# Dividing the neighbourhood attention's weights by their row sums: on GpSimd before the transposes, in place of diagonal matrices and ones products

## The chip, the cores and the metric

The kernel runs on one NeuronCore of a Trainium2 chip, as one launch. The metric is the time of one execution on the device, in microseconds (us). The five engines of a core run their own instruction queues in program order and wait for each other by semaphores: PE (TensorE, matmuls into PSUM), DVE (VectorE), ACT (ScalarE), POOL (GpSimd) and SP (which here issues most DMAs). GpSimd works only on SBUF in this kernel; PSUM is read by DVE and ACT.

## The reference, cut to what matters

The whole program is a small network: two layers that mix neighbourhood attention, differential attention and a convolution, and then feed-forward blocks with two other mixers. The change touches only the neighbourhood attention of the two layers, and there only the softmax's division:

```python
T, CTX, GRID_W, heads, dh = 512, 256, 64, 6, 64      # window of 8 rows x 16 columns
s_loc = einsum('bnqhd,bnkhd->bhnqk', q, k_window) + bias      # masked outside the window
s_ctx = einsum('bnqhd,bkhd->bhnqk', q, k_context)
p = softmax(concatenate([s_loc, s_ctx], axis=-1), axis=-1)
o = einsum('bhnqk,bnkhd->bnqhd', p[..., :nk], v_window) + einsum('bhnqk,bkhd->bnqhd', p[..., nk:], v_context)
y = concatenate([o * silu(gate), ...]) @ w_out
```

Layer 0 also computes a dense attention of the 256 context tokens over themselves in the same way; layer 1 does not. All of it is in float32.

## The kernel before, in words

`NaStage` does this attention, once in each of the two layers (`na0`, `na1`). Its work is cut into steps k = (p, b): p is one of three pairs of heads, and b is a block of 128 queries. Blocks b = 0 to 3 are latent queries against 256 keys of their window and the 256 context keys; b = 4 (layer 0 only) is the context, 256 queries against 256 keys, which has the same size of 128 partitions x 512 for each of the pair's two heads (i = 0, 1). Layer 0 has 15 steps, layer 1 has 12.

One step goes round all engines:

- **scores** (`scores_pe`, PE): queries times keys into two PSUM banks, 4 matmuls in the program.
- **max** (`max_dve`, DVE): adds the bias to the window's half and writes it to SBUF (`self.s[k % 3]`), and takes the row maxima. Its first instruction on the two heads is L1337 for b < 4, L1345 for b = 4.
- **exp** (`exp_act`, ACT, L1301): exponentials into `self.s[k % 3]`, with row sums in the small array `st`.
- **sums** (`sums_dve`, DVE, L1358 and L1360, or L1362 for b = 4): one over the row sums.
- **diag** (`diag_pool`, POOL, L1373): the identity matrix times one over the row sums, a diagonal matrix for each head (four 128x128 instructions for b = 4, else two).
- **turn** (`turn_pe`, PE, through the helper at L354): 8 transposes of the undivided weights, keys onto partitions, into banks 4 and 5.
- **copy** (`copy`, ACT L1285 for head 0, DVE L1287 for head 1): to SBUF, `self.pt[k % 2]`.
- **values** (`values_pe`, PE, through the helper at L345): first the ones products (a matrix of ones times the diagonal, which spreads one over the row sum of each query over 64 partitions in bank 7), then values times weights into bank 6.
- **out** (`out_dve`, DVE, L1387 and L1389): at the end of the latent blocks (b = 3) and for the context (b = 4), gate times bank 7, then times bank 6.

The order on each engine is written out by hand. PE's round k is values(k - 3), turn(k - 2), scores(k + 1). DVE's round k is max(k), sums(k - 1), out(k - 3), copy(k - 2). ACT's is copy(k - 2), exp(k). POOL does diag(k) for one k after another, and after k = 3 issues the DMA of the third pair's bias table. `self.s` has three buffers, `self.pt` has two, the score banks are two pairs. After the last step a fence has ACT, DVE and POOL wait for all others; PE goes on with the projections of the next stage, `LateStage`.

In the program a float32 product is one instruction; the trace shows two records for each.

Of the kernel before, what the change touches and what calls it, by code (L numbers as in the profile page):

```python
# [18 lines left out]
P = 128  # L19
# [171 lines left out]
def build(nc, ins, out_dram):  # L191
# [6 lines left out]
    with ctx:  # L198
# [946 lines left out]
        class NaStage:  # L1145
# [5 lines left out]
            def __init__(self, l, total, place, mix, norm, mod):  # L1151
                self.l, self.total, self.mix, self.tag, self.mod = l, total, mix, f"na{l}", mod
                self.norm = norm
                self.kT, self.qT, self.v = place.take(3, TA), place.take(3, TA), place.take(9, NA_W)
                self.s = [place.take(2, T) for _ in range(3)]
                self.pt = [place.take(2, T) for _ in range(2)]
                side = mix[:, 3:9, :].rearrange("p a b -> p (a b)")
                self.bias = [side[:, i * 1536:(i + 1) * 1536].rearrange("p (i b n) -> p i b n", i=2, b=3)
                             for i in range(2)]
                self.diag = [side[:, 3072 + i * T:3072 + (i + 1) * T].rearrange("p (a b) -> p a b", a=4) for i in range(3)]  # L1160
                names = lambda g: [(f"w_in{l}", i) for i in IN_PIECE[g]]
                self.k_of = Project(names(0), P, norm, TA)
                self.v_of = ByColumns(Project(names(1), P, norm, TA), self.v, [self.s[n][:, 0, :] for n in range(2)])
                self.g_of = Project(names(5), P, norm, total)
                self.q_of = Project(names(4), P, norm, total)
                self.steps = [(p, b) for p in range(3) for b in range(5 if total == TA else 4)]
                self.n = len(self.steps)
# [55 lines left out]
            def turn_pe(self, q, e, k):  # L1223

                for i in range(2):
                    q.wait_ge(*at(self.tag, "exp", k, i))
                    if k:
                        q.wait_ge(*at(self.tag, "copied", k - 1, i))
                    for j in range(4):
                        t = turned(e, banks[4 + i][:, j * P:(j + 1) * P], self.s[k % 3][:, i, j * P:(j + 1) * P])  # L1230
                    t.then_inc(*sig("na_turned", self.tag, "turned", k, i))

            def values_pe(self, q, e, k):
# [4 lines left out]
                    q.wait_ge(*at(self.tag, "out", k - 1))  # L1238
                if b == 4:
                    q.wait_ge(*at(self.tag, "out", k - 1))  # L1240
                q.wait_ge(*at(self.tag, "diag", k))
                for u in range(2 if b == 4 else 1):
                    c = (u if b == 4 else b) * P
                    for i in range(2):
                        mm(e, banks[7][64 * i:64 * i + 64, c:c + P], ones[:, 0:64],
                           self.diag[k % 3][:, 2 * i + u, :], True, True)
                tiles = self.TILES[b] + (7, 8) if b < 4 else (7, 8, 7, 8)
                for j, n in enumerate(tiles):
                    for i in range(2):
# [112 lines left out]
                    e.reciprocal(st[:, 12:16], st[:, 8:12]).then_inc(*sig("softmax"))  # L1362
                also(self.tag, "one over", k)

            def diag_pool(self, q, e, k):
                p, b = self.steps[k]
                st = self.st(k)
                q.wait_ge(*at(self.tag, "one over", k))
                if k >= 3:
                    q.wait_ge(*at(self.tag, "o", k - 3))  # L1370
                for n in range(2 if b < 4 else 4):
                    at4 = 2 * n if b < 4 else n
                    e.tensor_scalar(self.diag[k % 3][:, at4, :], ident, st[:, 12 + n:13 + n], None, MUL).then_inc(  # L1373
                        *sig("na_diag", self.tag, "diag", k))

            def out_dve(self, q, e, k):
                p, b = self.steps[k]
                if b < 3:
                    return
                q.wait_ge(*at(self.tag, "o", k))  # L1380
                if b == 3:
                    m = self.by_rows(self.mix[:, p, 0:T])
                    over, o = self.by_columns(banks[7]), self.by_columns(banks[6])
                else:
                    m = self.mix[:, p, T:TA]
                    over, o = banks[7][:, 0:TC], banks[6][:, 0:TC]
                e.tensor_tensor(m, over, m, MUL).then_inc(*sig("na_scaled"))  # L1387
                q.wait_ge(*last())
                e.tensor_tensor(m, o, m, MUL).then_inc(*sig("na_out", self.tag, "out", k))  # L1389


# [7 lines left out]
            def pool(self, q, e):  # L1399
                for p in range(2):  # L1400
                    q.wait_ge(*at(self.norm.tag, "lo", (len(spans(TA))) * DT - 1))
                    self.fetch_bias(q, e, p)
                for project in (self.k_of, self.v_of.p, self.g_of, self.q_of):
                    for n in project.pieces:
                        rest_of_weights(q, e, n)
                for k in range(self.n):
                    self.diag_pool(q, e, k)
                    if k == self.steps.index((0, 3)):
                        self.fetch_bias(q, e, 2)

# [2085 lines left out]
```

## Time and profile before

| | |
|---|---|
| median of 3 runs | 3389.8 us (3381.35 to 3390.28) |
| the profiled execution | 3391.12 us, of which its span of instructions 3389.3 us |
| PE busy, of the span | 3190.4 us, 94% |
| DVE busy | 1669.4 us, 49% |
| ACT busy | 1212.3 us, 36% |
| POOL busy | 748.7 us, 22% |
| the chain that ended last | PE 86%, DVE 7%, ACT 4%, POOL 1% |
| steps of `na0` | from 161.5 to 221.1 us of the span |
| steps of `na1` | from 743.3 to 792.3 us of the span |

The span is the stretch from the first to the last instruction of one profiled execution; the times in the rows below count from its start. The chain that ended last is followed back from the last instruction, at each step to what released it. The two stages of the change are 109 us of the 3389.3 us. Busy shares over the whole span say little on them: what counts is who waits for whom between 161.5 and 221.1 us and between 743.3 and 792.3 us.

### The profile page before, as it was taken

How to read it: one execution, taken by the hardware profiler on the slowest of the kernel's cores; microseconds unless marked ns; L12 is line 12 of the kernel's file. 1: busy time of each engine (PE TensorE's matmuls, PEld its weight loads, DVE VectorE, ACT ScalarE, POOL GpSimd, SP SyncE). 2: the span in 40 equal slices, each digit the busy share in tenths (PEclk: the TensorE clock that was granted, in tenths of full speed). 3: DMA queues.
4: the chain of work that ended last, by engine and by line, in shares of the span. 5: the costliest groups of instructions: out<-in, count | busy, mean ns of one | idle time of the engine just before them, and what ended most of it. 6: DMA issues, size and time to landing. Idle time of an engine off the chain costs nothing.

```text
span 3389.3 us, 39869 instructions
## 1 busy us (share of the span) xinstructions
PE 3190.4 (94%) x16156; PEld 2509.4 (74%) x16156; DVE 1669.4 (49%) x2507; ACT 1212.3 (36%) x2068; POOL 748.7 (22%) x578
## 2 busy tenths in 40 slices
PE   6999988899989999989899999999999999999998
PEld 4877667677767788867788778887888775578886
DVE  2256564426674534456665553446444425564344
ACT  3242265433273322232443332233222325542222
POOL 3234302334504000056332300001000343220000
PEclk8999999999999999999899999999999999999999
DMA  5213201221102232222000133232232231022322
GB/s 227 94 53 113 100 24 31 78 68 54 59 13 79 96 97 99 87 96 81 14 7 1 62 100 106 92 98 84 87 107 87 81 106 38 1 93 88 111 84 79
DMA packets 77575, 260.55 MB, mean 77 GB/s; under 512 B 8400, under 2 KB 9552, under 8 KB 76240
## 3 DMA queue, kind: packets, MB, share of 16 engines
q1 hardware_dynamic: 76528, 253.28, 22.8%
q0 software_dynamic: 864, 4.72, 0.4%
q8 instruction: 129, 2.11, 0.3%
q14 instruction: 54, 0.44, 0.0%
HBM read 255.87 MB, written 2.10 MB: 76 GB/s over the span
## 4 chain that ended last, share of the span: by engine, by line
PE 86%; DVE 7%; ACT 4%; POOL 1%; issue 1%; DMA 1%; SPq 0%; ACTq 0%; DVEq 0%; POOLq 0%
PE banks L345 84%; PE banks L354 2%; DVE area L576 1%; POOL w_lo L336 1%; DMA area<-in_w_mod 1%; DVE x_lat L579 1%; DVE small L1797 0%; DVE area L1741 0%; DVE area L1779 0%; ACT area L434 0%; POOL w_late L336 0%; ACT area L437 0%; ACT w_hi L326 0%; POOL area L410 0%; DVE area L494 0%
## 5 line engine op out<-in xcount | busy, mean ns | idle before, releaser
L345 PE MATMUL banks<-area,w_hi 128*128 128x512 f32 (+4 forms) x5896 | 1770.8, 383 | 22.7 <-ACT area L532 7.4
L345 PEld LDWEIGHTS banks<-area,w_hi 128*128 128x128 f32 (+2 forms) x5896 | 1078.5, 188 | 287.9 <-issue 22.6
L345 PE MATMUL banks<-area,w_lo 128*128 128x512 f32 (+4 forms) x2948 | 1120.2, 381 | 0.0
L345 PEld LDWEIGHTS banks<-area,w_lo 128*128 128x128 f32 (+2 forms) x2948 | 554.8, 188 | 118.8
L345 PE MATMUL banks<-area,w_late 128*128 128x512 f32 (+2 forms) x2316 | 580.8, 399 | 28.9 <-ACT area L532 14.8
L345 PEld LDWEIGHTS banks<-area,w_late 128*128 128x128 f32 (+1 forms) x2316 | 436.1, 191 | 146.9 <-ACT area L532 18.1
L326 ACT ACTIVATE w_hi<-w_raw 128x1024 fp32r<-128x1024 f32 (+2 forms) x361 | 349.7, 972 | 544.9 <-PE banks L345 416.3
L345 PE MATMUL banks<-area,area 64*128 64x256 f32 (+11 forms) x3464 | 419.0, 334 | 59.7 <-DMA area<-in_w_mod 15.9
L410 POOL TENSOR_TENSOR area<-area,area 128x512 f32<-128x512 f32 (+1 forms) x102 | 140.4, 1379 | 1475.2 <-ACT area L395 1473.5
L345 PEld LDWEIGHTS banks<-area,area 128*128 128x128 f32 (+4 forms) x3464 | 335.1, 183 | 134.1 <-issue 54.8
L336 POOL TENSOR_TENSOR w_lo<-w_raw,w_hi 128x1024 fp32r<-128x1024 f32 (+1 forms) x133 | 305.0, 2295 | 401.4 <-ACT w_hi L326 401.4
L336 DVE TENSOR_TENSOR w_lo<-w_raw,w_hi 128x1024 fp32r<-128x1024 f32 (+1 forms) x228 | 263.4, 1156 | 158.6 <-ACT w_hi L326 158.6
L969 ACT ACTIVATE area<-area 128x512 fp32r<-128x512 f32 x88 | 55.7, 632 | 419.1 <-DVE area L1000 419.1
L345 PE MATMUL banks<-area,const 128*128 128x512 f32 (+7 forms) x542 | 161.1, 454 | 35.6 <-DVE area L1061 7.6
L326 ACT ACTIVATE w_late<-w_raw 128x1024 fp32r<-128x1024 f32 (+2 forms) x103 | 100.9, 980 | 234.4 <-PE banks L345 230.9
L997 DVE TENSOR_TENSOR area<-banks,area 128x512 f32<-128x512 f32 x80 | 55.3, 691 | 240.2 <-PE banks L345 240.2
L1741 DVE SCALAR_TENSOR_TENSOR area<-area,par,area 128x783 f32<-128x783 f32 (+1 forms) x120 | 149.7, 1307 | 0.0
L345 PEld LDWEIGHTS banks<-area,const 128*128 128x128 f32 (+4 forms) x542 | 75.5, 180 | 96.4 <-issue 45.8
L862 DVE COPY area<-banks 128x512 f32<-128x512 f32 x72 | 46.9, 661 | 195.4 <-PE banks L345 179.1
L354 PE MATMUL banks<-const,area 128*128 128x128 f32 (+1 forms) x654 | 104.2, 287 | 34.8 <-DVE area L1791 21.3
L336 DVE TENSOR_TENSOR w_late<-w_raw,w_late 128x1024 fp32r<-128x1024 f32 (+1 forms) x76 | 86.1, 1133 | 85.3 <-ACT w_late L326 85.3
L354 PEld LDWEIGHTS banks<-const,area 128*128 128x128 f32 (+1 forms) x654 | 76.5, 146 | 57.3 <-issue 37.7
(236 smaller groups left out, 2309.2 us busy)
## 6 DMA issues: line engine op xcount, KB each, us to landing
w_raw<-in_l_ffn_w_in SPq DMA_DIRECT2D x176, 512.0 KB, 3.3
w_raw<-in_l_ffn_w_out SPq DMA_DIRECT2D x128, 384.0 KB, 3.0
w_raw<-in_w_in SPq DMA_DIRECT2D x66, 512.0 KB, 3.6
w_raw<-in_w_mod SPq DMA_DIRECT2D x32, 512.0 KB, 4.5
w_raw<-in_w_qkv SPq DMA_DIRECT2D x24, 512.0 KB, 3.3
w_raw<-in_l_w_in SPq DMA_DIRECT2D x22, 512.0 KB, 3.3
w_raw<-in_w_out SPq DMA_DIRECT2D x32, 320.0 KB, 2.9
area<-in_w_mod SPq DMA_DIRECT2D x8, 1024.0 KB, 16.5
```

What stands on the lines that cost most here:

```text
L326: e.activation(split_bufs(m)[0], raw_of(m), ACT.Copy).then_inc(*sig("w_rounded", "weights hi", m))
L336: e.tensor_tensor(lo, raw_of(m), hi.bitcast(f32), SUB).then_inc(*sig("w_split_dve" if dve else "w_split", "weights", m))
L345: return e.matmul(out, lhsT, rhs, start=first, stop=stop, skip_group_check=True)
L354: return e.transpose(out, in_, ident[0:k, 0:k])
L410: e.tensor_tensor(a, a, self.slot_of(s, j)[:, 0:c1 - c0], ADD).then_inc(*sig("squares_added", *self.tag, "added", s, j))
L576: e.scalar_tensor_tensor(y, y, self.gain(j, s), self.squares.rs[:, c0:c1], MUL, MUL).then_inc(*sig("post_step", self.tag, "step", s, j))
L579: e.tensor_tensor(x, x, y, ADD).then_inc(*sig("x_new", self.tag, "x", s, j))
L862: e.tensor_copy(yy, b).then_inc(*sig("evicted_dve", "evicted", u))
L969: e.activation(self.a_hi[:, j, :], a, ACT.Copy).then_inc(*sig("a_hi", self.tag, "a hi", half, j))
L997: e.tensor_tensor(a, bank, self.norm.rs, MUL).then_inc(*sig("evicted_dve", "evicted", u))
L1741: e.scalar_tensor_tensor(yy, uu, w, yy, MUL, ADD).then_inc(*sig("taps", self.tag, "tap", m, k))
```

## The change

The diagonal matrices and the ones products are gone. In place of diag(k), POOL multiplies the exponentials in `self.s[k % 3]` by one over their row sums, in place: two instructions of 128x512, or four of 128x256 for b = 4 (`scale_pool`, at L1366 of the changed kernel). The transposes of step k wait for this scaling, head by head, where they had waited for the exponentials. The values need neither the diagonals nor bank 7, and out is one multiplication by bank 6.

```diff
--- before.py
+++ after.py
@@ -1157,7 +1157,6 @@
                 side = mix[:, 3:9, :].rearrange("p a b -> p (a b)")
                 self.bias = [side[:, i * 1536:(i + 1) * 1536].rearrange("p (i b n) -> p i b n", i=2, b=3)
                              for i in range(2)]
-                self.diag = [side[:, 3072 + i * T:3072 + (i + 1) * T].rearrange("p (a b) -> p a b", a=4) for i in range(3)]
                 names = lambda g: [(f"w_in{l}", i) for i in IN_PIECE[g]]
                 self.k_of = Project(names(0), P, norm, TA)
                 self.v_of = ByColumns(Project(names(1), P, norm, TA), self.v, [self.s[n][:, 0, :] for n in range(2)])
@@ -1223,7 +1222,7 @@
             def turn_pe(self, q, e, k):
 
                 for i in range(2):
-                    q.wait_ge(*at(self.tag, "exp", k, i))
+                    q.wait_ge(*at(self.tag, "scaled", k, i))
                     if k:
                         q.wait_ge(*at(self.tag, "copied", k - 1, i))
                     for j in range(4):
@@ -1238,12 +1237,6 @@
                     q.wait_ge(*at(self.tag, "out", k - 1))
                 if b == 4:
                     q.wait_ge(*at(self.tag, "out", k - 1))
-                q.wait_ge(*at(self.tag, "diag", k))
-                for u in range(2 if b == 4 else 1):
-                    c = (u if b == 4 else b) * P
-                    for i in range(2):
-                        mm(e, banks[7][64 * i:64 * i + 64, c:c + P], ones[:, 0:64],
-                           self.diag[k % 3][:, 2 * i + u, :], True, True)
                 tiles = self.TILES[b] + (7, 8) if b < 4 else (7, 8, 7, 8)
                 for j, n in enumerate(tiles):
                     for i in range(2):
@@ -1362,16 +1355,15 @@
                     e.reciprocal(st[:, 12:16], st[:, 8:12]).then_inc(*sig("softmax"))
                 also(self.tag, "one over", k)
 
-            def diag_pool(self, q, e, k):
+            def scale_pool(self, q, e, k):
                 p, b = self.steps[k]
                 st = self.st(k)
                 q.wait_ge(*at(self.tag, "one over", k))
-                if k >= 3:
-                    q.wait_ge(*at(self.tag, "o", k - 3))
-                for n in range(2 if b < 4 else 4):
-                    at4 = 2 * n if b < 4 else n
-                    e.tensor_scalar(self.diag[k % 3][:, at4, :], ident, st[:, 12 + n:13 + n], None, MUL).then_inc(
-                        *sig("na_diag", self.tag, "diag", k))
+                for i in range(2):
+                    for u in range(2 if b == 4 else 1):
+                        s = self.s[k % 3][:, i, 256 * u:256 * u + 256] if b == 4 else self.s[k % 3][:, i, :]
+                        n = 12 + (2 * i + u if b == 4 else i)
+                        e.tensor_scalar(s, s, st[:, n:n + 1], None, MUL).then_inc(*sig("na_scaled", self.tag, "scaled", k, i))
 
             def out_dve(self, q, e, k):
                 p, b = self.steps[k]
@@ -1380,12 +1372,10 @@
                 q.wait_ge(*at(self.tag, "o", k))
                 if b == 3:
                     m = self.by_rows(self.mix[:, p, 0:T])
-                    over, o = self.by_columns(banks[7]), self.by_columns(banks[6])
+                    o = self.by_columns(banks[6])
                 else:
                     m = self.mix[:, p, T:TA]
-                    over, o = banks[7][:, 0:TC], banks[6][:, 0:TC]
-                e.tensor_tensor(m, over, m, MUL).then_inc(*sig("na_scaled"))
-                q.wait_ge(*last())
+                    o = banks[6][:, 0:TC]
                 e.tensor_tensor(m, o, m, MUL).then_inc(*sig("na_out", self.tag, "out", k))
 
 
@@ -1404,7 +1394,7 @@
                     for n in project.pieces:
                         rest_of_weights(q, e, n)
                 for k in range(self.n):
-                    self.diag_pool(q, e, k)
+                    self.scale_pool(q, e, k)
                     if k == self.steps.index((0, 3)):
                         self.fetch_bias(q, e, 2)
 
```

The names in the following rows: `area_79`, `area_80`, `area_81` are the three buffers of `self.s`; `area_59` holds the gates and, before, the diagonals; `area_76`, `area_77` are queries and keys, `area_78` the values, `area_82`, `area_83` the two buffers of `self.pt`; `s_na_scaled` is the semaphore of the scaling. First PE, in `na0`, one piece of the difference, from the first transposes to the second values:

```order
-L354 MATMUL banks<-const,area_79 128x128 x8
+L354 MATMUL banks<-const,area_79 128x128 [waits s_na_scaled]
+L354 MATMUL banks<-const,area_79 128x128 x3
+L354 MATMUL banks<-const,area_79 128x128 [waits s_na_scaled]
+L354 MATMUL banks<-const,area_79 128x128 x3
 L345 MATMUL banks<-area_76,area_77 128x256 [waits s_na_exp]
 L345 MATMUL banks<-area_76,area_77 128x256 x3
-L345 MATMUL banks<-area_59,const 64x128 [waits s_na_diag,s_na_copied_dve,s_na_copied_act]
-L345 MATMUL banks<-area_59,const 64x128
-L345 MATMUL banks<-area_82,area_78 64x128 x8
```

The transposes of step 0 now wait twice for POOL, once for each head, and the scores of step 3 stand behind them in PE's queue as before. The two ones products ahead of the values are gone.

Then POOL at the start of the steps of `na0`, before, behind the last weight of the projections:

```order
L336 TENSOR_TENSOR w_lo<-w_raw,w_hi 128x1024 [waits s_w_rounded] x11
L1373 TENSOR_SCALAR area_59<-const,small 128x128 [waits s_softmax]
L1373 TENSOR_SCALAR area_59<-const,small 128x128
L1373 TENSOR_SCALAR area_59<-const,small 128x128 [waits s_softmax]
L1373 TENSOR_SCALAR area_59<-const,small 128x128
```

and in the changed kernel:

```order
L336 TENSOR_TENSOR w_lo<-w_raw,w_hi 128x1024 [waits s_w_rounded] x11
L1366 TENSOR_SCALAR area_79<-area_79,small 128x512 [waits s_softmax]
L1366 TENSOR_SCALAR area_79<-area_79,small 128x512
L1366 TENSOR_SCALAR area_80<-area_80,small 128x512 [waits s_softmax]
L1366 TENSOR_SCALAR area_80<-area_80,small 128x512
```

The number of instructions on POOL and their place in its queue are the same; each has four times the columns, and reads and writes the buffer that PE is to transpose.

## Rows read from the trace of the kernel before

**Rows 1.** The page: the chain that ended last, share of the span by engine.

```profile
PE 86%; DVE 7%; ACT 4%; POOL 1%; issue 1%; DMA 1%; SPq 0%; ACTq 0%; DVEq 0%; POOLq 0%
```

**Rows 2.** Windows of both stages: stretch, busy us (instructions) by engine, clock.

```profile
161.50:221.10 59.60, 52.52 (x553) 41.31 (x553) 45.55 (x161) 37.11 (x135) 21.84 (x37) 0.97 0.05 15
743.30:792.30 49.00, 41.97 (x433) 33.02 (x433) 35.72 (x137) 29.91 (x108) 14.78 (x25) 0.97 0.05 18
```

**Rows 3.** Timeline of PE, `na0`: start us, us, engine, line [idle before <-releaser].

```profile
177.20 0.44 PE L345 MATMUL banks<-area,const 128*64 128x128 f32 x4
177.47 1.04 PE L345 MATMUL banks<-area,area 128*64 128x128 f32 x16
178.45 1.09 PE L354 MATMUL banks<-const,area 128*128 128x128 f32 x8
179.47 1.14 PE L345 MATMUL banks<-area,area 64*128 64x256 f32 x8
180.53 0.44 PE L345 MATMUL banks<-area,const 128*64 128x128 f32 x4
...
184.88 0.66 PE L345 MATMUL banks<-area,const 128*64 128x128 f32 x8 [0.94 <-DVE area L1287]
```

**Rows 4.** Timeline of DVE behind the scores that end at 180.61 us.

```profile
180.65 0.42 DVE L1337 CUSTOM_DVE_ANT_0 area<-banks,area 128x256 f32<-128x256 f32 x1 [0.38 <-PE banks L345]
...
182.51 0.15 DVE L1358 TENSOR_TENSOR small<-small 128x2 f32<-128x2 f32 x1
...
182.78 0.67 DVE L1387 TENSOR_TENSOR area<-banks,area 128x512 f32<-128x512 f32 x1
183.49 0.69 DVE L1389 TENSOR_TENSOR area<-banks,area 128x512 f32<-128x512 f32 x1
184.09 0.68 DVE L1287 COPY area<-banks 128x512 f32<-128x512 f32 x1
```

**Rows 5.** Timeline of POOL, `na0`: diag(0), the bias DMA, diag(5).

```profile
166.87 1.20 POOL L1373 TENSOR_SCALAR area<-const,small 128x128 f32<-128x128 f32 x2 [19.27 <-DVE small L1360]
...
177.18 0.60 POOL L1396 DMA_DIRECT2D area<-in_rpb  x1
...
182.96 1.19 POOL L1373 TENSOR_SCALAR area<-const,small 128x128 f32<-128x128 f32 x2 [1.15 <-DVE small L1360]
```

**Rows 6.** Line L1373 (diag): count, min/median/max ns, first and last start us, form.

```profile
L1373 POOL TENSOR_SCALAR area<-const,small x60: 594/605/609, 166.9 to 786.9; 128x128 f32<-128x128 f32 x60
```

**Rows 7.** Line L2969, another stage's in-place addition of a column on POOL.

```profile
L2969 POOL TENSOR_SCALAR area<-area,par x4: 1560/1566/1657, 1668.2 to 1673.0; 128x512 f32<-128x512 f32 x4
```

**Rows 8.** Line L1563, additions on POOL in `LateStage`.

```profile
L1563 POOL TENSOR_TENSOR area<-area,area x16: 1292/1788/1955, 289.1 to 922.1; 128x512 f32<-128x512 f32 x16
```

**Rows 9.** Timeline of PE, `na0`: turn(0), scores(3), values(0), values(14).

```profile
166.88 1.52 PE L354 MATMUL banks<-const,area 128*128 128x128 f32 x8
168.32 2.08 PE L345 MATMUL banks<-area,area 64*128 64x256 f32 x8
...
170.81 1.04 PE L345 MATMUL banks<-area,area 128*64 128x128 f32 x16
...
219.90 1.07 PE L345 MATMUL banks<-area,area 128*64 128x128 f32 x16
```

**Rows 10.** Timeline of PE and POOL, `na1`: values(0), values(11), diag(0).

```profile
752.92 1.07 PE L345 MATMUL banks<-area,area 128*64 128x128 f32 x16
...
791.09 1.07 PE L345 MATMUL banks<-area,area 128*64 128x128 f32 x16
...
748.72 1.19 POOL L1373 TENSOR_SCALAR area<-const,small 128x128 f32<-128x128 f32 x2 [8.76 <-DVE small L1360]
```

**Rows 11.** Windows of `na0`'s start and end: the last three are clock, DMA, GB/s.

```profile
166.00:170.00 4.00, 4.00 (x24) 2.80 (x22) 3.39 (x15) 4.00 (x17) 1.90 (x4) 0.67 0.00 0
...
210.00:221.00 11.00, 8.18 (x106) 6.80 (x102) 5.16 (x12) 4.34 (x15) 3.54 (x6) 1.00 0.01 1
```

**Rows 12.** Groups by line and shape, 140 to 290 us: max of b = 4.

```profile
L1345 DVE TENSOR_REDUCE small<-banks 128x2 f32<-128x512 f32 x6 | 4.1, 688 | 1.1 <-PE banks L345 1.1
```

## The prediction

> **What bounds the kernel now.** I read the page's chain first: it is 86% PE [rows 1], so a change counts where it changes when PE can go on. The two stages touched are 59.6 and 49.0 us long, and PE is busy for 52.5 and 42.0 us of them [rows 2]; POOL is busy for 21.8 and 14.8 us, so it has room, and the question is who would wait for it. Then one step on PE's timeline [rows 3]: ones products at 177.20, values at 177.47, transposes at 178.45, scores at 179.47, and the next step's ones products at 180.53. The step is 3.33 us with no idle time: values 0.98, transposes 1.02, scores 1.06, ones 0.27. PE is the bound of a plain step. It waits 0.94 us for DVE's copy once a head pair is finished, when DVE has both output multiplications (0.67 and 0.69 us) ahead of that copy [rows 3, 4].
>
> **What goes.** Ones products: 0.27 us of PE in each plain step. One output multiplication: 0.69 us of DVE at the end of each pair, most of the 0.94 us. Diagonals: 60 POOL instructions of 0.605 us [rows 6]. If nothing else changed, a step would be 3.06 us.
>
> **What comes, and its price.** POOL now works on 128x512 where it had 128x128, 48 times, and on 128x256 12 times. The trace before has no scaling of this buffer, so it is bounded: from below by 0.605 us, the same operation on a quarter of the columns [rows 6], which would mean that columns cost nothing; from above by four times that, 2.42 us, which would mean that only columns cost. The nearest row is an in-place operation with one column operand on 128x512, at 1.57 us in three of four cases and 1.66 in the other, while DVE was also at work [rows 7]. It is the same form of instruction and size, so I take P = 1.57 us, 3.14 for a step. Between 0.605 and 1.57, the 256-column form comes to 0.605 + 0.965/3 = 0.93, four of them 3.7 us.
>
> The GPSIMD Engine Reference of the Trainium skill (4.1, Engine selection) calls one-input work on GpSimd roughly line rate, and its section 3.1 gives 769 ns for 512 elements at best. The trace disagrees: 1566 ns [rows 7]. By the page's figure the sum would be that of the first rival below, by the row that of the forecast.
>
> **Where the new wait stands.** 3.14 us a step would fit on POOL beside a 3.33 us step. But POOL is now inside a loop. In PE's round k + 2 turn(k) waits for scale(k); behind it in PE's queue stand scores(k + 3). Scale(k) waits for sums(k), and DVE does sums(k) only after max(k + 1), which needs scores(k + 1). So from the end of scores(k + 1) to the end of scores(k + 3), two rounds:
>
> - to DVE's first instruction: 180.65 - 180.61 = 0.04 us; max until sums start: 182.51 - 180.65 = 1.86; sums until POOL starts: 182.96 - 182.51 = 0.45 [rows 4, 5]. (Scores end at 179.47 + 1.14 = 180.61 [rows 3].)
> - POOL: 3.14.
> - POOL's end to the first transpose: 0.11, taken from DVE's release of PE, since POOL releases none here: the copy ends at 184.09 + 0.68 = 184.77, the matmul starts at 184.88 [rows 3, 4]. Then half of the transposes, 0.51; scores to their end, 1.14 [rows 3].
>
> Sum: 0.04 + 1.86 + 0.45 + 3.14 + 0.11 + 0.51 + 1.14 = 7.25 for two rounds, 3.63 a round. In general a round is (4.11 + 2P)/2, unless PE's 3.06 or POOL's 2P is longer. So the loop, not PE and not POOL's occupancy, becomes the bound, and 0.27 us taken off PE turns into idle time of 0.57 us a round. Before, the transposes waited for exp alone, and diag only had to be there for the values a round later; nothing waited for it.
>
> **Sum over the stages.** All of it is on the path, since PE's later work starts where values(last) end.
>
> - Body of `na0`: values(0) to values(14) took 219.90 - 170.81 = 49.09 us [rows 9]; 14 rounds of 3.63 are 50.8: +1.7. The 49.09 hold the 0.94 us stalls, which the longer round swallows: after DVE's max and sums (1.86 + 0.27) one multiplication and a copy fit into 3.63 us.
> - The three context steps: 3.7 instead of 3.14 on POOL, in a loop of two rounds about +0.28 each, less what their shorter max gives (two of 0.69 [rows 12] for 1.86): +0.3 in all.
> - Body of `na1`: 791.09 - 752.92 = 38.17 us [rows 10]; 11 rounds are 39.9: +1.8.
> - Head of `na0`: POOL starts at 166.87 [rows 5], + 3.14 + 0.11 + 0.51 + 1.06 = 171.69 for values(0), which were at 170.81: +0.9. Head of `na1`: 748.72 + 4.82 = 753.54 for 752.92 [rows 10]: +0.6.
> - In the head the granted clock was 0.67 between 166 and 170 us [rows 11], at the 1.2 GHz level for part of it, after PE had waited for the first exponentials: transposes took 1.44 and scores 2.0 us to the next start [rows 9] where 1.02 and 1.06 are usual. PE will now wait longer there. If the half transposes and the scores go at the low level, that adds 0.21 + 0.95 to each head, 2.3 in all; if not, nothing. I take half: +1.2.
>
> Together +1.7 + 0.3 + 1.8 + 0.9 + 0.6 + 1.2 = +6.5 us.
>
> Costed at nothing: the bias DMA in POOL's queue, which was issued at 177.18 [rows 5] and now goes a few us later, is for step 10, whose max comes five rounds on; if it were late, each us would be on the path. Scaling in place needs no new buffer, and max(k + 3), which writes it, waits for turn(k) already. Weights of the next stage are split by POOL only behind the fence, which moves with the stage.
>
> DVE and POOL could disturb each other. POOL's 60 diagonals lie between 594 and 609 ns whatever DVE did [rows 6]; the additions at L1563, with two inputs, spread from 1.29 to 1.96 us, median 1.79 [rows 8]. SBUF — State Buffer of the Trainium skill (two separate sides) says that the two engines share a port pair held for a whole instruction, against a DVE operation in a two-port mode or with two inputs in SBUF. By that rule max, copy and out, which read PSUM and at most one input in SBUF, don't block POOL; by a rule that every overlap counts, the second rival would hold. The steady 594 to 609 agree with the page.
>
> The profiled execution took 3391.1 us, 1.3 above the median of the runs. 3391.1 + 6.5 = 3397.6; against the median 3389.8 + 6.5, so 3396.
>
> **Rivals.**
> 1. POOL is fast on wide rows (P below 1 us): the loop is 2.7 to 3.0 us, PE's 3.06 is the bound. 14 x 3.06 - 49.09 = -6.2, 11 x 3.06 - 38.17 = -4.5, head -0.5; in five rounds DVE (1.86 + 0.27 + 0.67 + 0.67 and its waits, some 3.5) holds PE up by 0.4: +2. Together -9.2, 3381. For it: one input only. Against: the 1.57 us of rows 7. Chance 0.07.
> 2. POOL is slowed by DVE, P = 1.79 as in rows 8. Round 3.85: +4.8, +4.2, heads +2.4, context 0.3, clock 1.2, together +12.9: 3403. For it: POOL's instructions will now always overlap with DVE's. Against: the tight spread of rows 6. Chance 0.15.
> 3. Slower by POOL's occupancy, P = 2.42, four times rows 6: 2P = 4.83 is over the loop's (4.11 + 4.83)/2 = 4.47, and POOL sets the round. This decides from P = 2.06 on. 14 x 4.83 - 49.09 = +18.5, 11 x 4.83 - 38.17 = +15.0, heads +4.9, with the clock some +40: 3430. Against: rows 7 again. Chance 0.05.
> 4. The clock falls through the stage, since PE idles 0.57 us a round: transposes and scores of a loop take 1.16 us more, 0.58 a round, 25 x 0.58 = +14.5 on top: 3410. Against: between 210 and 221 us PE was busy for only 8.2 of 11 us and kept 1.00 [rows 11]. Chance 0.08.
>
> **Numbers.** Forecast 0.65, with a range of its own from 3391 to 3402. What this kernel's measurement can tell from no change is 0.3%, 10 us: 3380 to 3400. Slower than that: rival 2 mostly (0.12), 3 and 4 (0.11), and 0.05 of the forecast's upper part: 0.28. Faster: rival 1 where it goes past its 9.2 us, 0.05. Within: 0.67. The range of 8 in 10 leaves out rivals 1 and 3 and most of 4: 3388 to 3409.
>
> **What would show it.** Right: L1366 at about 1.57 us, starting 0.45 us after sums start; PE's plain rounds at 3.6 to 3.7 us, with a gap ahead of the second half of the transposes that is released by POOL; no 0.94 us wait for DVE's copy; the two stages 6 us longer in sum and all others as they were. Wrong: L1366 well off 1.57; rounds of 3.06 us; a granted clock under 0.9 in the body; or gaps ahead of the values instead of the transposes.

## The result, and the profile after

The changed kernel takes 3395.1 us (median of 20 runs, 3389.17 to 3398.33), the kernel before 3389.8 us (median of 20). The ratio is 1.0019, with a 95% interval of 1.0012 to 1.0026: slower by 0.19%, some 6 us, clear of noise but within the 0.3% that the prediction calls no change. Forecast were 3396 us and rounds bound by a loop through POOL. (A round is what PE does for one step: values, transposes, scores.)

Line L1366 in the profile after (count, min/median/max ns, first and last start, forms; then who waited for it, us and times):

```profile
L1366 POOL TENSOR_SCALAR area<-area,small x60: 912/1562/1572, 166.4 to 795.2; 128x512 f32<-128x512 f32 x48, 128x256 f32<-128x256 f32 x12
...
who waited for it (us, times):
  PEld banks L354: 16.5, 24
  PE banks L354: 9.8, 22
```

The scaling takes what the other in-place row promised [rows 7]. For diag nobody had waited; now the transposes wait for this line in most rounds. Two rounds of PE's timeline in `na0` (start us, us, line, [idle before <-releaser]), which answer to [rows 3]:

```profile
202.85 0.66 PE L354 MATMUL banks<-const,area 128*128 128x128 f32 x4
203.88 0.66 PE L354 MATMUL banks<-const,area 128*128 128x128 f32 x4 [0.37 <-POOL area L1366]
204.47 2.16 PE L345 MATMUL banks<-area,area 64*128 64x256 f32 x24
206.56 0.66 PE L354 MATMUL banks<-const,area 128*128 128x128 f32 x4
207.41 0.66 PE L354 MATMUL banks<-const,area 128*128 128x128 f32 x4 [0.20 <-POOL area L1366]
207.99 2.16 PE L345 MATMUL banks<-area,area 64*128 64x256 f32 x24
210.08 0.66 PE L354 MATMUL banks<-const,area 128*128 128x128 f32 x4
```

The transposes fall into two halves. Between the halves PE waits for the second head's scaling. From 202.85 to 210.08 two rounds take 7.23 us, where the sum said 7.25. The third row of 24 records holds scores(k + 1) and, without ones products between, values.

The stage's landmarks on PE, read from several stretches of its timeline: scores(0), values(0) (the first records of it), values(14), the next stage:

```profile
161.10 2.00 PE L345 MATMUL banks<-area,area 64*128 64x256 f32 x16 [0.78 <-DVE area L1307]
...
172.65 0.70 PE L345 MATMUL banks<-area,area 128*64 128x128 f32 x4
...
223.17 1.09 PE L345 MATMUL banks<-area,area 128*64 128x128 f32 x16 [0.83 <-issue]
224.37 0.73 PE L345 MATMUL banks<-area,w_hi 128*128 128x512 f32 x2
```

From scores(0) to the next stage `na0` takes 63.27 us. Before, the same stretch went from 161.53 to 221.07, 59.54 us. Taken apart, with `na1` measured in the same way:

| us | `na0` before | after | `na1` before | after |
|---|---|---|---|---|
| head, scores(0) to values(0) | 9.28 | 11.55 | 9.54 | 11.54 |
| body, values(0) to the last values | 49.09 | 50.52 | 38.17 | 40.00 |
| to the next stage | 1.17 | 1.20 | 1.18 | 1.19 |
| whole | 59.54 | 63.27 | 48.89 | 52.73 |

The first stretch is called the head of the stage here, the second its body. Heads +4.3, bodies +3.3, together +7.6 us: 108.4 before, 116.0 after. In the heads the clock was low for longer than in [rows 11]. Windows of `na0`'s head in the profile after (the third number from the end is the granted clock):

```profile
165.00:168.00 3.00, 1.14 (x8) 0.69 (x8) 2.67 (x14) 2.20 (x10) 1.57 (x2) 0.88 0.00 0
168.00:171.00 3.00, 2.52 (x10) 1.79 (x12) 1.06 (x5) 1.80 (x6) 3.00 (x2) 0.50 0.01 3
171.00:174.00 3.00, 3.00 (x22) 2.18 (x22) 1.64 (x6) 0.68 (x4) 1.62 (x2) 0.50 0.00 0
174.00:177.00 3.00, 3.00 (x32) 2.29 (x32) 2.05 (x8) 1.96 (x8) 1.93 (x2) 0.99 0.00 0
```

PE had worked 1.14 of 3 us before 168, waiting first for exp and then for POOL, and then had the 1.2 GHz level until about 174 us.

The profiled execution shows only 0.6 us more span, 3389.9, for stages that are 7.6 us longer. What lies behind `na1` is 6.6 us shorter in this profile, 2590.4 us for 2597.0, with the same code. Of these, 4.4 us are in one stage. Its scan on DVE, before and then after:

```profile
L2910 DVE TENSOR_TENSOR_SCAN area<-area,area x4: 1268/1928/3011, 1668.7 to 1836.3; 128x512 f32<-128x512 f32 x4
```

```profile
L2900 DVE TENSOR_TENSOR_SCAN area<-area,area x4: 1260/1928/3008, 1675.5 to 1838.7; 128x512 f32<-128x512 f32 x4
```

The four scans span 167.6 us in the one and 163.2 in the other, at a mean granted clock of 0.96 and 0.99 between 1668 and 1838 us. Single profiled executions therefore differ by some 4 us in code that the change does not touch. For what follows, the length of the two stages in the profile is the sharp measure (the changed kernel profiled a second time gave 116.0 again), and the median over the runs is the blunt one.

### The profile page after: what moved, and what is told of

Its sections match the earlier page's. It is cut to its first block, busy times and chain, and to the rows that moved or that the text cites. A ratio compares the mean times of both kernels' runs of the same rounds, so it can differ in the third digit from the quotient of the medians.

```text
span 3389.9 us, 39592 instructions
## 1 busy us (share of the span) xinstructions
PE 3186.4 (94%) x16036; PEld 2496.4 (74%) x16036; DVE 1665.2 (49%) x2498; ACT 1211.7 (36%) x2068; POOL 796.7 (24%) x578
## 4 chain that ended last, share of the span: by engine, by line
PE 83%; DVE 8%; ACT 3%; POOL 3%; issue 1%; DMA 1%; SPq 0%; ACTq 0%; DVEq 0%; POOLq 0%
PE banks L345 81%; PE banks L354 2%; POOL area L1366 1%; DVE area L576 1%; DVE x_lat L579 1%; POOL w_lo L336 1%; DVE area L538 1%; DMA area<-in_w_mod 1%; DVE small L1787 0%; DVE area L1731 0%; DVE area L1769 0%; ACT area L434 0%; POOL w_late L336 0%; ACT area L437 0%; ACT w_hi L326 0%
## 5 line engine op out<-in xcount | busy, mean ns | idle before, releaser
L345 PEld LDWEIGHTS banks<-area,area 128*128 128x128 f32 (+4 forms) x3464 | 328.3, 180 | 148.7 <-issue 68.0
L345 PE MATMUL banks<-area,const 128*128 128x512 f32 (+4 forms) x422 | 150.0, 504 | 25.3 <-DVE area L1061 7.6
L345 PEld LDWEIGHTS banks<-area,const 128*128 128x128 f32 (+3 forms) x422 | 70.2, 195 | 78.5 <-issue 34.5
```

Of the source, the lines that this page charges most:

```text
L345: return e.matmul(out, lhsT, rhs, start=first, stop=stop, skip_group_check=True)
```

## The experiments

Theory L (loop): a round of PE is half of the 7.25 us from scores(k + 1) to scores(k + 3) by way of DVE and POOL, (4.11 + 2P)/2 with P the duration of one scaling, and at least PE's own work. Rivals: O (occupancy), POOL's busy time sets the round; C (contention), POOL and DVE slow each other; and that what was removed was worth little. Three runs leave computation out and only price things: no scaling and scaling beside do not divide at all, half the columns divides half of each row. All others compute the whole. A table first; "stages" is the sum of both, from scores(0) to the next stage. Intervals are of the ratio to the kernel before, run beside each.

| kernel | stages, us | median, us | ratio (95% interval) |
|---|---|---|---|
| before | 108.4 | 3389.8 | |
| changed | 116.0 | 3395.1 | 1.0019 (1.0012 to 1.0026) |
| no scaling | 99.3 | 3378.3 | 0.9972 (0.9962 to 0.9982) |
| scaling beside | 100.6 | 3379.7 | 0.9979 (0.9970 to 0.9988) |
| half the columns | 102.8 | 3381.1 | 0.9978 (0.9969 to 0.9986) |
| sums between | 106.6 | 3382.4 | 0.9983 (0.9974 to 0.9991) |
| sums last | 151.6 | 3429.1 | 1.0120 (1.0106 to 1.0134) |
| deeper | 106.3 | 3390.5 | 0.9999 (0.9991 to 1.0008) |
| filler | 112.3 | 3396.9 | 1.0024 (1.0015 to 1.0033) |
| between and filler | 104.3 | 3381.7 | 0.9979 (0.9970 to 0.9989) |
| before, filler | 108.5 | 3388.6 | 1.0000 (0.9991 to 1.0009) |
| changed, again | 116.0 | 3395.9 | 1.0025 (1.0015 to 1.0035) |
| filler, again | 113.8 | 3396.4 | 1.0028 (1.0016 to 1.0040) |
| split | 103.5 | 3376.9 | 0.9976 (0.9965 to 0.9987) |

**No scaling.**

```diff
-                    q.wait_ge(*at(self.tag, "scaled", k, i))
+                    q.wait_ge(*at(self.tag, "exp", k, i))
...
-                    self.scale_pool(q, e, k)
```

> The changed kernel with POOL's scaling left out (so the division by the row sums is not done) and the transposes waiting for exp again. It prices what the change removes, with nothing put in its place. Loop theory (the wait for POOL inside the two-round loop and the slow heads cost what they cost, the removal is worth its full 0.27 us a round): PE's rounds 3.06 us, longer only in the five rounds with an output multiplication; some 9 us under the kernel before, about 3381. Rival (the ones products were hidden in waits anyway, so their removal is worth little): rounds stay near 3.3 us, 3388 to 3390.

Measured: 3378.3 us, stages 9.1 us shorter than before. Rounds in a row:

```profile
198.52 1.09 PE L354 MATMUL banks<-const,area 128*128 128x128 f32 x8
199.54 2.16 PE L345 MATMUL banks<-area,area 64*128 64x256 f32 x24
201.63 1.09 PE L354 MATMUL banks<-const,area 128*128 128x128 f32 x8
202.65 2.16 PE L345 MATMUL banks<-area,area 64*128 64x256 f32 x24
204.74 1.09 PE L354 MATMUL banks<-const,area 128*128 128x128 f32 x8
```

A plain round is 3.11 us for 3.33 before, so the ones products were worth 0.22 us a round, not the 0.27 of the sum, and PE's own bound is 3.11, not 3.06. Where an output multiplication is due, a round is 3.62 us for 4.56 (`na0`) and 4.34 (`na1`): there DVE's second multiplication went too. The bodies are 8.1 us shorter, the heads 1.1. The rival that the removal was hidden anyway falls.

**Scaling beside.** The wait as in the first, a wait for the scaling ahead of values, and POOL on a buffer of its own (it also waits for its own last write there):

```diff
-                        s = self.s[k % 3][:, i, 256 * u:256 * u + 256] if b == 4 else self.s[k % 3][:, i, :]
+                        s = self.idle[:, i, 256 * u:256 * u + 256] if b == 4 else self.idle[:, i, :]
-                        e.tensor_scalar(s, s, st[:, n:n + 1], None, MUL).then_inc(*sig("na_scaled", self.tag, "scaled", k, i))
+                        e.tensor_scalar(s, C("cos")[:, 0:s.shape[-1]], st[:, n:n + 1], None, MUL).then_inc(*sig("na_scaled", self.tag, "scaled", k, i))
```

> The same, but POOL does instructions of the same number and size as in the changed kernel, from a constant table into a buffer that nobody reads; the transposes wait for exp, only the values wait for POOL, a round later (the division is left out). Loop theory: as e1, within 2 us of it, L1366's successor at 1.57 us and DVE's instructions as long as before. Rival one (POOL and DVE disturb each other): POOL's instructions or DVE's max are longer than 1.6 and 0.42 us and the time is 3 us or more above e1. Rival two (POOL's occupancy, 3.14 us a round, is the bound): rounds of 3.14 to 3.2 instead of 3.06, 2 to 3 us above e1.

Measured: stages 100.6 us, 1.3 over no scaling, time 3379.7. POOL's line in that profile:

```profile
L1370 POOL TENSOR_SCALAR area<-const,small x60: 914/1557/1573, 165.8 to 779.4; 128x512 f32<-128x512 f32 x48, 128x256 f32<-128x256 f32 x12
...
who waited for it (us, times):
  PE banks L345: 1.2, 1
```

The same POOL work, done beside, makes PE wait once, for 1.2 us. POOL's times are those of the changed kernel, and DVE's first instruction of max takes 419 ns here, in the kernel before and in the changed one. C falls, and O as the cause of the 3.63 us rounds: what costs is not that POOL works but that the transposes need it.

**Half the columns.**

```diff
-                        s = self.s[k % 3][:, i, 256 * u:256 * u + 256] if b == 4 else self.s[k % 3][:, i, :]
+                        s = self.s[k % 3][:, i, 256 * u:256 * u + 128] if b == 4 else self.s[k % 3][:, i, 0:256]
```

> The changed kernel with half of the columns scaled (the context half of each row is not divided), the waits as they are. P is 0.93 us. Loop theory: (4.11 + 1.86) / 2 = 2.99, under PE's 3.06, so PE bounds again and only the heads' extra wait stays, some 1.3 us each less than with 1.57: 3383 to 3386. Rival (it is having to wait for POOL at all, through the semaphore and the broken run of transposes, not its duration): rounds stay near 3.5 us and the time near 3394.

Measured: 3381.1 us, 2 under the forecast range, stages 102.8. The first transposes of rounds stand 3.11 us apart, 3.62 where an output multiplication is due, as without any scaling; scaling takes 0.925 us. The rival that a wait on POOL costs whatever its length falls.

**Sums between.** DVE's order alone is changed:

```diff
-                    if 1 <= k <= self.n:
+                    if k == self.n:
                         self.sums_dve(q, e, k - 1)
...
                 for i in range(2):
+                    if i and k:
+                        self.sums_dve(q, e, k - 1)
```

> The changed kernel with the same work, but DVE does sums(k - 1) between the two heads of max(k) in place of behind both. POOL can start 0.93 us earlier in every round, no engine has less to do. Loop theory: 7.25 - 0.93 = 6.32 for two rounds, 3.16 a round, and POOL's 3.14 stands close behind it: bodies 14 x 3.2 and 11 x 3.2 us, some 7 to 9 us less than the changed kernel together, heads as slow: 3387 to 3389. Rival (POOL's occupancy or PE's waits for DVE set the 3.63 us rounds): no change from 3395, or slower since the second head's max is later.

Measured: 3382.4 us, better than forecast; it keeps the whole computation. The first transposes of rounds in `na1`:

```profile
754.88 1.09 PE L354 MATMUL banks<-const,area 128*128 128x128 f32 x8
...
758.00 1.18 PE L354 MATMUL banks<-const,area 128*128 128x128 f32 x8
...
761.21 1.23 PE L354 MATMUL banks<-const,area 128*128 128x128 f32 x8
...
764.46 0.66 PE L354 MATMUL banks<-const,area 128*128 128x128 f32 x4
...
768.15 1.09 PE L354 MATMUL banks<-const,area 128*128 128x128 f32 x8
```

Plain rounds of `na1` are 3.11 to 3.25 us for the 3.16 worked out, and 3.63 to 3.69 where an output multiplication is due, which the forecast's 3.2 for all rounds did not count. The stages are 9.4 us shorter than the changed kernel's: 6.9 in the bodies (83.6 us, where 3.2 a round would be 80.0) and 2.5 in the heads. Of the latter, 1.4 are the clock's: in `na1` it was at 0.78 between 750 and 754 us, where the changed kernel had 0.50 and 0.57 from 752 to 762. Against the kernel before the stages are 1.8 us shorter, so some 4 of the 6 us under it are not in the stages and may be chance. O falls again: no engine got less to do.

**Sums last**, the same in the other direction:

```diff
-                    if 1 <= k <= self.n:
-                        self.sums_dve(q, e, k - 1)
                     if k >= 3:
                         self.out_dve(q, e, k - 3)
                     if 2 <= k < self.n + 2:
                         self.copy(q, e, k - 2, 1)
+                    if 1 <= k <= self.n:
+                        self.sums_dve(q, e, k - 1)
```

> The changed kernel with DVE's sums(k - 1) moved behind copy(k - 2); each engine does the same work in the same number of instructions. Loop theory: sums(k) now waits for a copy that waits for turn(k - 1), and scale(k) waits for sums(k), so the loop closes within one round: copy 0.69, sums 0.45, POOL 3.14, 0.11, half of the transposes 0.57, together 4.96 us a round in place of 3.63; 25 rounds are +33 us, about 3428, and POOL's instructions stay 1.57 us. Occupancy theory (POOL's 3.14 us or PE's work set the round): the order on DVE doesn't matter, 3395 to 3398.

Measured: 3429.1 us for the forecast 3428. PE's timeline, rounds in a row:

```profile
200.30 0.66 PE L354 MATMUL banks<-const,area 128*128 128x128 f32 x4 [0.88 <-POOL area L1366]
200.89 2.16 PE L345 MATMUL banks<-area,area 64*128 64x256 f32 x24
203.67 0.66 PE L354 MATMUL banks<-const,area 128*128 128x128 f32 x4 [0.62 <-POOL area L1366]
205.21 0.65 PE L354 MATMUL banks<-const,area 128*128 128x128 f32 x4 [0.89 <-POOL area L1366]
205.79 2.16 PE L345 MATMUL banks<-area,area 64*128 64x256 f32 x24
208.58 0.66 PE L354 MATMUL banks<-const,area 128*128 128x128 f32 x4 [0.62 <-POOL area L1366]
```

From 203.67 to 208.58 is 4.91 us; the loop within one round was worked out as 4.96. This run tells the theories apart by 33 us, and L holds. The stages are 35.6 us longer than the changed kernel's, 2.6 over the 33. Here PE idles 1.5 us in a round and the granted clock does fall in the bodies, to 0.54 between 232 and 247 us and between 822 and 836.

**Deeper.** `self.s` gets a fourth buffer, `side[:, 3072:4096]`, all `k % 3` become `k % 4`, and PE, ACT and DVE do a step's later parts a round later; on PE:

```diff
-                for k in range(self.n + 3):
-                    if k >= 3:
-                        self.values_pe(q, e, k - 3)
-                    if 2 <= k < self.n + 2:
-                        self.turn_pe(q, e, k - 2)
+                for k in range(self.n + 4):
+                    if k >= 4:
+                        self.values_pe(q, e, k - 4)
+                    if 3 <= k < self.n + 3:
+                        self.turn_pe(q, e, k - 3)
```

> The changed kernel with a fourth buffer for the exponentials (where the diagonals had been) and transposes, copies and values of a step one round later. The loop then spans three rounds, 7.25 / 3 = 2.4, and what is left is POOL's own 3.14 us a round (3.7 for the context steps) and PE's 3.06. Loop theory: rounds of about 3.15 us, the bodies 7 to 9 us shorter than the changed kernel's, some of it given back in filling and draining a longer pipeline, 3386 to 3391. Rival (POOL to PE latency is paid in each round whatever the depth): rounds stay at 3.6 and the time is above 3395.

Measured: 3390.5 us, stages 106.3. Rounds in a row, and one with an output multiplication of both kinds behind it:

```profile
192.82 1.09 PE L354 MATMUL banks<-const,area 128*128 128x128 f32 x8
193.84 2.16 PE L345 MATMUL banks<-area,area 64*128 64x256 f32 x24
195.93 1.09 PE L354 MATMUL banks<-const,area 128*128 128x128 f32 x8
...
205.89 1.09 PE L354 MATMUL banks<-const,area 128*128 128x128 f32 x8
208.28 1.09 PE L345 MATMUL banks<-area,area 128*64 128x128 f32 x16 [1.30 <-DVE area L1281]
```

Plain rounds are 3.11 to 3.5 us, with nine short waits for POOL of 1.6 us in all, and the bodies 10.6 us shorter than the changed kernel's for the forecast 7 to 9. Part is given back: a first turn 8.17 us after scores(0) where the changed kernel has 6.95, and waits for DVE's copy of up to 1.30 us. The stages end 2.1 us under before's, and the medians show none of it (ratio 0.9999).

**Filler**, in the changed kernel, then with sums between, then in the kernel before:

```diff
+            def fill(self, e, n):
+                for _ in range(n):
+                    mm(e, banks[7][:, 0:256], ident, C("cos")[:, 0:256], True, True)
...
+                    if k == 0:
+                        self.fill(e, 1 if i else 3)
...
+                if k == 2:
+                    self.fill(e, 4)
```

> The changed kernel with matmuls of the identity with a constant table into an unused bank in the gaps of each stage's head: four ahead of scores(2), three and one ahead of the two halves of turn(0), 128x256 each. They leave the result as it is. Clock theory (the heads lose some 2 us each because the granted clock falls to half while PE waits and stays there until about 174 us): the clock stays near 1.00, transposes and scores of the head go at 1.02 and 1.06 us, 3 to 5 us less, 3391. Rival (the heads lose because turn(0) waits for POOL, and the clock is a small part): within 1 us of 3395.

> The filler of the run before on top of sums between the two heads of max. If both gains are what they are taken for (a shorter loop, and a head at full clock), they add up: the two stages 3 to 5 us shorter than with sums between alone, 3378 to 3381. If the filler holds up work that was ready, or the clock was not the head's cost: no better than sums between alone, 3382 to 3384.

> The kernel before with the same filler matmuls in the heads as in the two filler runs. In the kernel before, the clock was 0.53 between 168 and 171 us; turn(0) and scores(3) lose 1.4 us there in each stage. Clock theory (a head at half clock costs about that, and filling it gives it back): the two stages 2 to 3 us shorter than before's 108.4, the time 3386 to 3388. Rival (what the head gains is waited off in the body, or lost elsewhere, as the first filler run's time says, in which the stages were 3.7 us shorter than the changed kernel's and the time was no better): 3389 to 3391, with the stages shorter or not.

> The changed kernel with the filler in the heads once more. The first time its two stages were 112.3 us for the changed kernel's 116.0, and its time 3396.9 for 3395.1. If the 3.7 us are real and the time was chance (downstream stages that differ by a few us from execution to execution): 3391 to 3393 now. If the filler costs elsewhere what it gives here: 3395 to 3398 again, with the stages at 112.

Measured in the changed kernel: the same head windows as above read

```profile
168.00:171.00 3.00, 2.54 (x26) 1.82 (x27) 1.29 (x4) 2.27 (x9) 3.00 (x3) 1.00 0.01 3
171.00:174.00 3.00, 3.00 (x35) 2.29 (x33) 2.58 (x10) 1.99 (x8) 1.96 (x2) 1.00 0.00 0
```

and the stages are 3.7 and 2.2 us shorter in two profiles. The turn and scores(3) of `na0`'s head, in the changed kernel and then with the filler:

```profile
169.59 1.12 PE L354 MATMUL banks<-const,area 128*128 128x128 f32 x4 [0.43 <-POOL area L1366]
170.64 3.78 PE L345 MATMUL banks<-area,area 64*128 64x256 f32 x24
```

```profile
168.64 0.66 PE L354 MATMUL banks<-const,area 128*128 128x128 f32 x4 [0.46 <-POOL area L1374]
169.22 2.16 PE L345 MATMUL banks<-area,area 64*128 64x256 f32 x24
```

The heads are 1.4 us shorter each in both profiles, 2.8 together: that is what the low level cost there. The first profile gains another 0.9 us in `na1`'s body, whose start the low level had reached too (0.57 between 756 and 762 us in the changed kernel). The second loses 1.5 us against it in `na1`'s last rounds, with a granted clock of 0.89 between 785 and 800 us for 1.00. But the program is no faster (3396.9 and 3396.4, beside 3395.1 and 3395.9 for the changed kernel). The forecast of 3391 missed; the second run came out where its expectation had put the case that the filler costs elsewhere what it gives here. The clocks of all executions show part of it. The windows of the heads alone (from 0.95 to 1.00 over 160 to 226 us, from 0.92 to 1.00 over 740 to 802) would raise the mean granted clock of the program by 0.0024. Over all executions it is 0.9785 and 0.9788 with the filler and 0.9782 and 0.9781 without. So most of the low-level time is not gone but lies elsewhere. In the first filler profile it does: 0.94 between 1600 and 2000 us, where the changed kernel had 0.97, with a scans' stage of 167.6 us. The second has 0.97 and 163.3 us there. Why the low level turns up elsewhere stays open.

In the kernel before, the filler gained nothing: its head took 9.47 us for 9.28. There turn(0) had been ready early, and the seven fillers ahead of it held it up for as long as the clock had cost. On top of sums between, the stages are 2.3 us shorter, for the forecast 3 to 5, and the medians 0.7 apart, which is no difference.

**The changed kernel again.**

> The changed kernel once more, on the same chip and beside the filler run below, to compare the two directly: 3394 to 3397, the two stages 116 us together.

Measured: 3395.9 us and 116.0, as expected. The span of this profile is 3394.1 us, 4.2 over the first one's, with both stages as long as there.

**Split.** On top of sums between and the filler; POOL's share of the second head ends at column 256, and the rest is DVE's:

```diff
+                    if 1 <= k <= self.n:
+                        self.scale_dve(q, e, k - 1)
...
+            def scale_dve(self, q, e, k):
+                p, b = self.steps[k]
+                s, n = self.s[k % 3][:, 1, 256:512], 12 + (3 if b == 4 else 1)
+                q.wait_ge(*at(self.tag, "one over", k))
+                e.tensor_scalar(s, s, self.st(k)[:, n:n + 1], None, MUL).then_inc(*sig("na_scaled_dve", self.tag, "scaled by dve", k))
```

> Sums between the two heads of max, the filler, and one quarter of each step's scaling (128x256 of the second head) moved from POOL to DVE, behind max. POOL has 2.5 us a round instead of 3.14, DVE about 0.25 more, in all 3.0. Loop theory: POOL no longer stands close behind PE, rounds of 3.06 to 3.1 us, the stages 101 to 103 us for the 104.4 of the run with filler and sums between, the time 3379 to 3382. Rival (DVE's extra operation is in the way of copies and max, or shares POOL's port): rounds of 3.2 or more, or POOL's instructions over 1.6 us, no gain on 3382.

Measured: 3376.9 us, ratio 0.9976 (0.9965 to 0.9987), the lowest time with the whole computation kept; stages 103.5. It beats both kernels. The stages account for 5.0 us of 13 between the medians, or of 8 by the ratio; its interval overlaps those of sums between, alone and with the filler, so of these three none is shown to be best. DVE's part took 345 ns. But the rounds did not come down to the forecast 3.06 to 3.1 us: the bodies are 82.6 us, and 82.7 with sums between and the filler alone. What PE waited for in `na0` and in `na1` in that run (us in total, times, the longest):

```profile
PE banks L345 <- DVE area L1288: 2.1, 3, 0.9
PE banks L354 <- POOL area L1376: 1.6, 4, 0.9
...
PE banks L345 <- DVE area L1288: 3.1, 4, 0.9
PE banks L354 <- POOL area L1376: 0.8, 3, 0.4
```

and with the split:

```profile
PE banks L345 <- DVE area L1290: 4.3, 5, 1.1
...
PEld banks L354 <- POOL area L1386: 0.3, 2, 0.2
...
PE banks L345 <- DVE area L1290: 4.4, 6, 0.9
```

The waits for POOL are all but gone, and those for DVE's copy (L1288, L1290) grew from 5.2 to 8.7 us. So the rival of the expectation, that DVE's extra operation is in the way of its copies, came in for the bodies, and the 0.9 us by which the stages are shorter are in the heads.

## Why the prediction was right

- *POOL's duration.* P = 1.57 was forecast, 1.562 measured. The Trainium skill's GPSIMD Engine Reference gives 769 ns for 512 elements at best (section 3.1) and calls one-input work roughly line rate (4.1, Engine selection); the measurement is twice its figure. The 256-column form took 0.925 us for the forecast 0.93.
- *The loop.* 3.63 us a round were worked out; the bodies give 50.52/14 = 3.61 and 40.00/11 = 3.64, and two rounds in the middle 7.23 for 7.25. Shown by moving one DVE step both ways: 0.93 us less in the loop took 6.9 us off the bodies, with plain rounds of 3.11 to 3.25 for 3.16, and the loop closed within one round gave 4.91 for 4.96.
- *The bodies.* +1.4 and +1.8 us for the forecast +2.0 (with the context steps) and +1.8.
- *The removal.* Real and on the path: 9.1 us without any scaling, where the first rival's arithmetic had 9.2. The sum matches better than its parts: 0.22 us a plain round for the 0.27 worked out, and up to 0.94 where an output multiplication is due. The waits of 0.94 us for DVE's copy in mid-stage are gone, as forecast; in the last rounds of both stages waits of 0.87 us for it remain.
- *The heads.* +0.9 and +0.6 for the wait and +1.2 for the clock were forecast, +4.3 measured. The wait was right: with the filler the heads are 10.15 us, 0.9 and 0.6 over before's 9.28 and 9.54. (It compares a head at full clock with one that had itself lost 0.4 us in its turn and 0.9 in its scores to the low level [rows 9].) The clock's term was mis-sized: I took half of 2.3 us, and 2.8 were paid. The low level lasted past turn(0) and scores(3). Half of the transposes cost 0.47 us more by it, for the 0.21 of the sum (which I had from a turn that was only partly at the low level), and the scores 0.95, as in the sum.
- *The sum.* +6.5 forecast, +7.6 in the stages, +5.3 between the medians (6 by the ratio). Part of that match is luck: bodies 0.5 under the forecast, the clock's term 1.6 over it, and the excess of the stages is offset by what differs elsewhere.
- *Rivals.* None came in. Contention: POOL's line at 1.55 to 1.57 us beside a busy DVE, and no cost in the run with the scaling beside. The clock stayed at 1.00 through the bodies of the changed kernel, but for their first 1.5 and 3 us, with PE idle 0.2 to 0.9 us at a time; with sums last, where it idles 1.5 us a round, it fell to 0.54 in stretches of the bodies.

## What to carry to other kernels

Work moved to an idle engine costs nothing only while nobody in a loop waits for it: before asking whether it fits beside the others' time, follow the chain from one use of the buffer back to the same engine, count the rounds that it spans, and divide. Then the cheapest repair is to shorten that chain: here two tiny DVE instructions done 0.93 us earlier turned a loss of 7.6 us in the stages into a gain of 1.8. And where a stage is 3% of a program, compare its own length in the traces beside the medians, and the granted clock beside both.

## What the runs showed of the hardware that I had not expected

A multiplication by one column on POOL took 605 ns for 128 columns, 925 for 256 and 1562 for 512: 2.5 ns a column on some 285 ns. It was the same in place and from a table into another buffer (1562 and 1557 ns), and at most 1573 ns beside a DVE that took its large operands from PSUM. Beside DVE's own scaling from SBUF to SBUF (split), 4 of 57 were longer: three of 256 columns with 948 to 1087 ns and one of 512 with 1725.

Executions of one kernel differ by some 10 us, and the granted clock goes with it. Of the 22 executions of the kernel before that were run beside the split, the five fastest (3383.5 to 3384.6 us) had a mean granted clock of 0.980 to 0.982, the six slowest (3392.1 to 3392.8) one of 0.977 or 0.978.

The stage of the scans, with unchanged code, was 167.5 to 167.8 us long in eight profiles and 161.6 to 163.3 in six. In 13 of the 14 these lengths lie in bands by when its first scan starts, whatever the kernel: 163.3 us for the three starts from 1656.9 to 1660.7, 167.5 to 167.7 for the seven from 1663.1 to 1674.5, and 161.6 to 163.3 for the three from 1675.5 to 1678.1. (Sums last, far behind at 1715.4, has 167.8.) If the start decides, a change that moves a later stage by a few us gains or loses 4 us there. No run moved that start alone, so this is a pattern and not a shown cause.

And PE at full clock in the heads, 2.8 us gained there by the traces, did not show in the time of the program.
